# Hybrid decoder layer with a hierarchical MoE: the weight ring's last two places exchanged, the ninth chunk no longer held back, three gather buffers moved

## The chip, the cores and the metric

The kernel runs on one core of a Trainium2 chip. The time is the device time of one execution in microseconds. A core has five engines with instruction streams of their own: TensorE (PE), VectorE (DVE), ScalarE (ACT), GpSimd (POOL) and SyncE (SP). SyncE computes nothing here and issues DMAs. Sixteen DMA engines move data between HBM and the on-chip memory; SyncE's DMAs go through one queue (q1 in the profile) and GpSimd's through another (q0).

## What is computed

One layer for 512 prompt tokens and 8 sample tokens, all with 1024 features. A mixer with a recurrent and an attention branch gives `x1`; then comes a mixture of experts, with the top 1 of 4 groups and the top 2 of the 8 experts in it:

```
x1 = layer_norm(ALPHA * x + merged @ w_o, ln1_g, ln1_b)
g_logits = xf @ w_group + b_group                      # top 1 of 4
e_logits = (xf @ w_router + b_router)                  # 8 per group, top 2
...
def expert_block(args):
    xi, e = args
    h = jax.nn.silu(xi @ w_gate[e]) * (xi @ w_up[e])
    return h @ w_down[e]
...
y = layer_norm(ALPHA * x1 + ff, ln2_g, ln2_b)
```

All values are float32. Each of the 32 experts has three matrices of 2 MB (1024 x 512, 1024 x 512 and 512 x 1024), 201 MB together.

## The kernel before

The program is written out engine by engine, and all order between engines is made with semaphores. It has two stages around the change.

**The mixer** ends at about 504 us with the product `w_o`. Its result, before the norm, is `zT` (features on the partitions). TensorE transposes it into `zn`, which has the tokens on the partitions (semaphore `s_zt`), and multiplies it by the router's weights (`s_lg`, "logits"). ScalarE normalises the five token tiles in place (`s_x1` counts them), and GpSimd stores each to `x1_half` in HBM (`s_x1o` counts 16 for each store that has landed). Meanwhile VectorE works through the routing, a chain of small instructions that ends in tables: `s_oh10` counts slot one-hots, `s_tabc` the tables that are ready (the first is `tabG`, which tells which rows an expert gathers).

**The experts.** For expert e, GpSimd gathers the rows of its tokens from `x1_half` into one of four buffers `xg`, VectorE scales them by `g1` and `b1`, TensorE transposes them, VectorE copies the result to `xt`, and TensorE multiplies by gate and up (`gate_up`, in two halves), and by down (`down`) one expert later. The results are scattered to `ff_half`. Tables always cover 64 tokens per expert, as half rows.

**The weight ring.** The 96 weight chunks of 2 MB go through a ring of 11 places `slot[0]` to `slot[10]` of 16384 bytes per partition, at the bottom of on-chip memory. A chunk is half of gate and up together (two DMAs of 1 MB) or a whole down matrix. `load(n)` on SyncE issues chunk n; from n = 11 on it first waits until TensorE has read the chunk that lay there. So the first eleven loads depend on TensorE only through the mixer's buffers, which lie at the same addresses, and chunk 11 waits for the first half of expert 0's `gate_up`:

```
def load(n):
    if n >= RING:
        sp.wait_ge(*read_by(n - RING))
```

Of the places, `slot[8]` lies over `zT`, `slot[9]` and the lower part of `slot[10]` over the routing's temporaries (`rt(...)`, handed out from `oG` upwards), and the upper part of `slot[10]` over `zn`. The gather buffers `xg` lie above the ring, over the rows of `zn`, so they are cleared (`memset`) only after the stores of x1 have landed. SyncE issues its DMAs in program order, and a wait holds back all behind it.

Of the kernel before, what the change touches and what calls it, by code (L numbers as in the profile page):

```python
# [18 lines left out]
F32 = mybir.dt.float32  # L19
F32R = mybir.dt.float32r  # L20
BF16 = mybir.dt.bfloat16
U32 = mybir.dt.uint32
# [5 lines left out]
P = 128  # L28
# [6 lines left out]
TT = 5  # L35
# [4 lines left out]
NG, EPG = 4, 8  # L40
NE = NG * EPG
NL = NG + NE
# [3 lines left out]
CAP = 64  # L46
NOV = 16
NBLK = NE + NOV
# [4 lines left out]
NXG = 4  # L53
RING = 11
SLOT = 16384
# [88 lines left out]
def build(nc, A, O):  # L144
    ctx = ExitStack()
    with ctx:
        base = 16512

        def at(name, shape, dt, off):
            return nc.alloc_sbuf_tensor_at(name, shape, dt, offset=base + off)  # L150

        def sem(name):
            return ctx.enter_context(nc.semaphore(name))
# [5 lines left out]
        oE, oF, oG, oH, oI, oJ = 126720, 139840, 148224, 189184, 172800, 205568  # L159
# [80 lines left out]
        ro = [oG]  # L240

        def rt(name, shape, dt=F32):
            n = 1
            for s in shape[1:]:
                n *= s
            t = at(name, shape, dt, ro[0])
            ro[0] += (n * (2 if dt == BF16 else 4) + 31) // 32 * 32
            return t
        lg, lt = rt("lg", [P, TT, NL]), rt("lt", [P, TT, NL])
        lgG, lgE = lg[:, :, 0:NG], lg[:, :, NG:NL]  # L250
        io4 = rt("io4", [P, NG])
        io32 = rt("io32", [P, NE])
        ioM = rt("ioM", [P, TT, NE])
        io64 = rt("io64", [P, CAP])
        io48 = rt("io48", [P, NBLK])
        io16 = rt("io16", [P, NOV])
        tri = rt("tri", [P, P])
        triB = rt("triB", [P, P], BF16)
        oneB = rt("oneB", [P, P], BF16)
        tokv = rt("tokv", [P, 2, 2, TT])  # L260
        off = rt("off", [P, 1])
        w5 = [rt(f"w5{n}", [P, TT]) for n in range(5)]
        w10 = [rt(f"w10{n}", [P, 2, TT]) for n in range(6)]
        g20 = [rt(f"g20{n}", [P, TT, NG]) for n in range(2)]
        e320 = [rt(f"e320{n}", [P, 2 * TT, NE]) for n in range(2)]
        esel = rt("esel", [P, TT, NE])
        hot = rt("hot", [P, 2, TT, NE])
        hotB = rt("hotB", [P, TT, NE], BF16)
        cum = rt("cum", [P, 4, NE])
        ov16 = rt("ov16", [P, NOV, NE])  # L270
        bkE = rt("bkE", [P, 2 * TT, NBLK])
        tabG = at("tabG", [P, NBLK], U32, oK + 3040)
        tabD = at("tabD", [P, NBLK], U32, oK + 3232)
        tabW = at("tabW", [P, NBLK], F32, oK + 3424)
        ovT = at("ovT", [P, NOV + 1], I32, oK + 3616)
        ovf = at("ovf", [P, NOV + 1], F32, oK + 3712)
        rk = rt("rk", [P, 2 * TT, CAP])
        bk = rt("bk", [P, 2 * TT, 3, NBLK])
        assert ro[0] <= oI

        slot = [at(f"slot{n}", [P, 8, 512], F32, SLOT * n) for n in range(RING)]
        oX = RING * SLOT
        oX = RING * SLOT
        xt = [at(f"xt{n}", [P, 512], F32, oX + 2048 * n) for n in range(2)]
        gu = [at(f"gu{n}", [P, 512], F32, oX + 4096 + 2048 * n) for n in range(2)]
        xg = [at(f"xg{n}", [P, 512], F32, oX + 8320 + 2048 * n) for n in range(NXG)]
        g1, b1 = [at(n, [P, 512], F32, oX + 16512 + 2048 * k) for k, n in enumerate(("g1", "b1"))]
        sgm = [at(f"sgm{n}", [P, 4, CAP], F32, oX + 20608 + 1024 * n) for n in range(2)]
        hT = [at(f"hT{n}", [P, 4, CAP], F32, oX + 22656 + 1024 * n) for n in range(2)]
        idG = [at(f"idG{n}", [P, 1], U32, oX + 24704 + 32 * n) for n in range(NXG)]  # L290
        idD = [at(f"idD{n}", [P, 1], U32, oX + 24832 + 32 * n) for n in range(2)]

        f0 = [at(f"f0{n}", [P, D], F32, 4096 * n) for n in range(TT)]
        f1 = [at(f"f1{n}", [P, D], F32, 4096 * (TT + n)) for n in range(TT)]
# [59 lines left out]
        s_hot, s_pre, s_oh10, s_tab, s_tabc, s_tabo = sem("one_hots"), sem("ranks"), sem("slot_one_hots"), sem("tables"), sem("tables_kept"), sem("overflow_table")  # L354
# [69 lines left out]
        def read_by(n):  # L424

            e, c = CHUNKS[n]
            return (s_guh, s_gup, s_yp)[c], e + 1
# [7 lines left out]
        def _(sp):  # L435
# [59 lines left out]
# [4 lines that stand above are left out]
                chunk(CHUNKS[n][1], CHUNKS[n][0], slot[n % RING], s_wx[n % RING])  # L499

            def chunk(c, e, dst, signal):

                if c < 2:
                    for n, w in enumerate(("w_gate", "w_up")):
                        src = A[w][bass.ds(e, 1), c * (D // 2):(c + 1) * (D // 2), :].rearrange("e (p j) f -> p (e j f)", p=P)
                        sp.dma_start(dst[:, 4 * n:4 * n + 4, :].rearrange("p j f -> p (j f)"), src).then_inc(signal, 16)  # L506
                else:
                    src = A["w_down"][bass.ds(e, 1), :, :].rearrange("e (p j) d -> p (e j d)", p=P)
                    sp.dma_start(dst[:, :, :].rearrange("p a b -> p (a b)"), src).then_inc(signal, 16)  # L509
# [28 lines left out]
            load(7)  # L538
            sp.wait_ge(s_zt, 4)
            sp.wait_ge(s_lg, 1)  # L540
            sp.wait_ge(s_x1o, 16 * TT)
            load(8)
            sp.wait_ge(s_tabc, 4)
            for n, name in enumerate(("ln2_g", "ln2_b")):
                sp.dma_start(vec32[n * KT:(n + 1) * KT, :], A[name].rearrange("(k n) -> k n", n=P)).then_inc(s_l2, 16)
            load(9)
            load(10)

            for n in range(RING, 3 * NE - 1):
# [35 lines left out]
        def _(pool):  # L585
            gp = nc.gpsimd
            pc = [0]

            def link(ins):

                pc[0] += 1
                ins.then_inc(p_c, 1)
                pool.wait_ge(p_c, pc[0])
# [88 lines left out]
            pool.wait_ge(s_rcst, 10)  # L682
            gp.memset(off[CAP:P, :], float(FARAWAY + 1)).then_inc(s_rcst, 1)
            pool.wait_ge(s_rcst, 11)
            for m, n in enumerate(ORDER):
                pool.wait_ge(s_x1, m + 1)
                pool.dma_start(x1_rows[n * P:n * P + ROWS[n], :].rearrange("t (c n) -> t c n", c=4),
                               zn[m][P - ROWS[n]:P, :, :]).then_inc(s_x1o, 16)
            pool.wait_ge(s_x1o, 16 * TT)
            for j in range(NXG):  # L690
                link(gp.memset(xg[j][:, :], 0.0))
            pool.wait_ge(s_tabc, 1)

            def fetch(dst, index, signal):
# [1315 lines left out]
```

## Time and profile before

| | |
|---|---|
| median of 3 runs | 1030.9 us (1029.38 to 1034.28) |
| profiled execution, whole | 1030.14 us |
| its span (first to last instruction) | 1028.3 us |
| PE busy | 886.4 us, 86% of the span |
| DVE busy | 447.9 us, 44% |
| ACT busy | 280.7 us, 27% |
| POOL busy | 117.6 us, 11% |
| HBM read and written | 257.36 MB and 15.16 MB |

Times in the trace count from the start of the span. A row of a timeline has the start, the duration, the engine, the line of the kernel and the tiles that are written and read; in square brackets stand the engine's idle time before it and what ended it. "SPq" is SyncE's own sequence of DMA issues; such a row is the issue alone, not the transfer.

### The profile page before, as it was taken

The numbers are of one execution on the slowest core, as the hardware profiler recorded it, in microseconds if no ns is written. First come the engines' busy times: TensorE is split into PE (matmuls) and PEld (weight loads), VectorE is DVE, ScalarE is ACT, GpSimd is POOL, SyncE is SP. The second block draws the span as 40 slices with busy tenths as digits, with TensorE's granted clock in tenths as the row PEclk, the third lists the DMA queues.
The fourth block names the chain that finished last, engine by engine and source line by source line (L and its number), as shares of the span: only waits on it lengthen the run. The fifth ranks groups of instructions, "written<-read, shape, count | busy, mean of one in ns | idle before, by whom it ended". The sixth has DMA issues, their size and how long they took to land.

```text
span 1028.3 us, 14537 instructions
## 1 busy us (share of the span) xinstructions
PE 886.4 (86%) x5897; PEld 615.0 (60%) x5897; DVE 447.9 (44%) x922; ACT 280.7 (27%) x537; POOL 117.6 (11%) x202
## 2 busy tenths in 40 slices
PE   6899999899999999999749999997777877777870
PEld 6789999789899989998733333332332322322330
DVE  3865876774555645442462232332212212222207
ACT  3667544345344422211311111111010110110113
POOL 2000300000000010030130122211111111111110
PEclk9999999989999999999959999999999999999995
DMA  9324621212122232439389999999999999999946
GB/s 285 113 62 82 189 78 63 81 42 83 48 77 82 51 81 85 121 137 415 145 332 419 423 421 422 424 420 423 425 420 423 424 422 422 423 421 423 422 174 232
DMA packets 85957, 263.16 MB, mean 256 GB/s; under 512 B 28767, under 2 KB 59643, under 8 KB 65250
## 3 DMA queue, kind: packets, MB, share of 16 engines
q1 hardware_dynamic: 78850, 246.94, 61.9%
q0 software_dynamic: 7040, 15.28, 4.0%
q8 instruction: 47, 0.77, 0.3%
q14 instruction: 20, 0.16, 0.0%
HBM read 257.36 MB, written 15.16 MB: 265 GB/s over the span
## 4 chain that ended last, share of the span: by engine, by line
PE 43%; SPq 27%; DMA 13%; DVE 10%; ACT 3%; issue 3%; POOL 1%; POOLq 0%; DVEq 0%; ACTq 0%
PE ps L768 28%; SPq L506 22%; PE ps L1065 5%; SPq L509 4%; PE ps L1092 4%; DMA slot<-in_w_up 3%; DMA xg<-x_half,idG 3%; DMA ff_half<-xg,idD 2%; DMA raw<-in_w_o 2%; DMA raw<-in_w_in 1%; PE ps L894 1%; PE ps L884 1%; DVE rawL L1418 1%; PE ps L860 1%; DVE hL L1499 1%
## 5 line engine op out<-in xcount | busy, mean ns | idle before, releaser
L1065 PE MATMUL ps<-slot,xt 128*64 128x512 f32 x512 | 231.9, 600 | 47.6 <-DMA slot<-in_w_up 46.8
L1066 PE MATMUL ps<-slot,xt 128*64 128x512 f32 x512 | 232.4, 601 | 0.0
L1065 PEld LDWEIGHTS ps<-slot,xt 128*64 128x64 f32 x512 | 66.4, 137 | 184.4 <-issue 139.7
L768 PE MATMUL ps<-xTh,wh 128*128 128x260 f32 x704 | 147.0, 290 | 4.0 <-DVE rawL L1418 4.0
L768 PE MATMUL ps<-xTl,wh 128*128 128x260 f32 x704 | 143.1, 285 | 0.0
L768 PE MATMUL ps<-xTh,rawL 128*128 128x260 f32 x704 | 143.1, 285 | 0.0
L1092 PE MATMUL ps<-slot,hT 128*64 128x512 f32 x512 | 116.9, 597 | 19.1 <-issue 17.7
L1418 DVE TENSOR_TENSOR rawL<-raw,wh 128x1024 fp32r<-128x1024 f32 x68 | 84.1, 1240 | 81.7 <-ACT wh L1150 81.6
L768 PEld LDWEIGHTS ps<-xTh,wh 128*128 128x128 f32 x704 | 110.0, 192 | 9.9 <-issue 9.1
L768 PEld LDWEIGHTS ps<-xTl,wh 128*128 128x128 f32 x704 | 110.2, 191 | 0.0
L768 PEld LDWEIGHTS ps<-xTh,rawL 128*128 128x128 f32 x704 | 109.9, 191 | 0.0
L1341 ACT ACTIVATE gu<-ps 128x512 f32<-128x512 f32 x32 | 19.1, 597 | 284.7 <-PE ps L1066 284.7
L1150 ACT ACTIVATE wh<-raw 128x1024 fp32r<-128x1024 f32 x68 | 71.3, 1051 | 74.5 <-PE ps L768 47.9
L1899 DVE COPY xt<-ps 128x512 f32<-128x512 f32 x32 | 22.1, 691 | 148.9 <-PE ps L1049 148.9
L1092 PEld LDWEIGHTS ps<-slot,hT 128*64 128x64 f32 x512 | 38.0, 136 | 75.8 <-issue 72.9
L1906 DVE SCALAR_TENSOR_TENSOR xg<-ps,tabW,xg 128x512 f32<-128x512 f32 x32 | 24.0, 750 | 123.5 <-PE ps L1092 123.5
L1066 PEld LDWEIGHTS ps<-slot,xt 128*64 128x64 f32 x512 | 66.4, 137 | 0.0
L702 POOL DMA_INDIRECT ff_half<-xg,idD x32 | 32.8, 1025 | 171.4 <-DVE xg L1906 162.5
L1891 DVE TENSOR_TENSOR xg<-xg,g 128x512 f32<-128x512 f32 x32 | 22.1, 691 | 63.4 <-DMA xg<-x_half,idG 63.4
L1352 ACT ACTIVATE sgm<-ps 128x256 f32<-128x256 f32 x32 | 12.3, 383 | 136.4 <-PE ps L1077 136.4
L656 POOL TENSOR_TENSOR zT<-xTh,xTl 128x520 f32<-128x520 f32 x8 | 13.1, 1660 | 275.8 <-PE ps L894 206.9
L1235 ACT ACTIVATE sS<-sS,nm 128x256 f32<-128x256 f32 (+1 forms) x64 | 30.1, 471 | 46.1 <-DVE es L1538 46.1
(316 smaller groups left out, 1243.0 us busy)
## 6 DMA issues: line engine op xcount, KB each, us to landing
slot<-in_w_gate SPq DMA_DIRECT2D x64, 1024.0 KB, 30.5
slot<-in_w_up SPq DMA_DIRECT2D x64, 1024.0 KB, 31.5
slot<-in_w_down SPq DMA_DIRECT2D x31, 2048.0 KB, 33.0
raw<-in_w_in SPq DMA_DIRECT2D x18, 1024.0 KB, 5.2
raw<-in_w_in SPq DMA_DIRECT2D x16, 256.0 KB, 4.4
raw<-in_w_lru_out SPq DMA_DIRECT2D x4, 1024.0 KB, 4.8
raw<-in_w_attn_out SPq DMA_DIRECT2D x16, 256.0 KB, 4.5
raw<-in_w_o SPq DMA_DIRECT2D x4, 1024.0 KB, 5.2
```

The lines of the kernel that those rows point to most:

```text
L506: sp.dma_start(dst[:, 4 * n:4 * n + 4, :].rearrange("p j f -> p (j f)"), src).then_inc(signal, 16)
L509: sp.dma_start(dst[:, :, :].rearrange("p a b -> p (a b)"), src).then_inc(signal, 16)
L702: pool.indirect_dma_start(out=ff_half, out_offset=bass.IndirectOffsetOnAxis(ap=index[:, 0:1], axis=0), in_=src[:, :], in_offset=None, boun ...
L768: last = mm(out_of[:, a, 0:HT], w[:, k, :], x[:, k, a * HT:(a + 1) * HT], start=(k == 0 and n == 0), stop=(k == KT - 1 and n == 2))
L1065: mm(out[0:CAP, :], tokens, w[:, q, :], start=start, stop=stop)
L1066: last = mm(out[CAP:P, :], tokens, w[:, 4 + q, :], start=start, stop=stop)
L1092: last = mm(out[a * CAP:(a + 1) * CAP, :], h[:, q, :], w_down[:, 2 * q + a, :], start=(q == 0), stop=(q == 3))
L1150: sc.activation(whi(t), wcol(t, raw), ACT.Copy).then_inc(s_hi, 1)
L1235: sc.activation(sS[hh][:, j, lo:256], sS[hh][:, j, lo:256], ACT.Exp, bias=nm[:, hh, j:j + 1], accum_out=dn[:, hh, j:j + 1]).then_inc(s_ex, 1)
L1418: v.tensor_tensor(wcol(t, rawL), wcol(t, raw), whi(t).bitcast(F32), ALU.subtract).then_inc(s_lo, 1)
L1891: v.tensor_tensor(x, x, g1[:, :], ALU.mult).then_inc(s_xs, 1)
L1906: v.scalar_tensor_tensor(out=x, in0=bank[5 + e % 3], scalar=tabW[:, e:e + 1], in1=x, op0=ALU.mult, op1=ALU.add).then_inc(s_ye, 1)
```

## The change

Three things are edited.

1. The places of chunks 9 and 10 are exchanged in memory: `slot[9]` now lies at the tenth position from zero (over `zn` and some routing temporaries), `slot[10]` below it. The routing's temporaries are handed out in another order, so that those that die early lie under `slot[9]`.
2. On SyncE `load(8)` no longer waits for `s_x1o`. That wait, and one for the second slot one-hot, now stand ahead of `load(9)`, and `load(9)` stands ahead of the wait for the tables instead of behind it.
3. Three of the four `xg` buffers, `g1` and `b1` lie above the rows of `zn`. GpSimd clears those three ahead of the stores of x1, and the fourth after them.

```diff
+        cum = rt("cum", [P, 4, NE])
+        ...
+        io4 = rt("io4", [P, NG])
+        assert ro[0] <= 10 * SLOT
+        ro[0] = 10 * SLOT
+        lg, lt = rt("lg", [P, TT, NL]), rt("lt", [P, TT, NL])
...
-        slot = [at(f"slot{n}", [P, 8, 512], F32, SLOT * n) for n in range(RING)]
+        slot = [at(f"slot{n}", [P, 8, 512], F32, SLOT * (n if n < 9 else 19 - n)) for n in range(RING)]
...
-        xg = [at(f"xg{n}", [P, 512], F32, oX + 8320 + 2048 * n) for n in range(NXG)]
+        xg = [at(f"xg{n}", [P, 512], F32, oX + (15104 + 2048 * n if n < 3 else 12288)) for n in range(NXG)]
...
             sp.wait_ge(s_lg, 1)
+            load(8)
             sp.wait_ge(s_x1o, 16 * TT)
-            load(8)
+            sp.wait_ge(s_oh10, 2)
+            load(9)
             sp.wait_ge(s_tabc, 4)
             for n, name in enumerate(("ln2_g", "ln2_b")):
                 sp.dma_start(vec32[n * KT:(n + 1) * KT, :], A[name].rearrange("(k n) -> k n", n=P)).then_inc(s_l2, 16)
-            load(9)
             load(10)
...
             pool.wait_ge(s_rcst, 11)
+            for j in range(NXG - 1):
+                link(gp.memset(xg[j][:, :], 0.0))
             for m, n in enumerate(ORDER):
                 pool.wait_ge(s_x1, m + 1)
                 pool.dma_start(x1_rows[n * P:n * P + ROWS[n], :].rearrange("t (c n) -> t c n", c=4),
                                zn[m][P - ROWS[n]:P, :, :]).then_inc(s_x1o, 16)
             pool.wait_ge(s_x1o, 16 * TT)
-            for j in range(NXG):
-                link(gp.memset(xg[j][:, :], 0.0))
+            link(gp.memset(xg[NXG - 1][:, :], 0.0))
```

On SyncE's queue, from the chunk `slot7` on, before the change (the number behind a tile's name is that of its buffer, and in brackets stand the semaphores that the instruction waits for, by their long names: `x1_stored` is `s_x1o`, `tables_kept` is `s_tabc`):

```order
L509 DMA slot7_185<-in_w_down 128x4096
L506 DMA slot8_186<-in_w_gate 128x2048 [waits x1_stored,logits,z_T]
L506 DMA slot8_186<-in_w_up 128x2048
L545 DMA vec32_131<-in_ln2_g 8x128 [waits tables_kept]
L545 DMA vec32_131<-in_ln2_b 8x128
L506 DMA slot9_187<-in_w_gate 128x2048
L506 DMA slot9_187<-in_w_up 128x2048
L509 DMA slot10_188<-in_w_down 128x4096
L506 DMA slot0_178<-in_w_gate 128x2048 [waits gate_up_half]
```

The same place of SyncE's queue with the change (`slot_one_hots` is `s_oh10`):

```order
L511 DMA slot7_185<-in_w_down 128x4096
L508 DMA slot8_186<-in_w_gate 128x2048 [waits logits,z_T]
L508 DMA slot8_186<-in_w_up 128x2048
L508 DMA slot9_187<-in_w_gate 128x2048 [waits slot_one_hots,x1_stored]
L508 DMA slot9_187<-in_w_up 128x2048
L549 DMA vec32_131<-in_ln2_g 8x128 [waits tables_kept]
L549 DMA vec32_131<-in_ln2_b 8x128
L511 DMA slot10_188<-in_w_down 128x4096
L508 DMA slot0_178<-in_w_gate 128x2048 [waits gate_up_half]
```

The wait for x1 has moved from chunk 8 to chunk 9, and chunk 9 has passed the two small loads and their wait for the tables. Chunk 10 stays where it was.

On GpSimd, from its last constant to the first gather, before the change:

```order
L683 MEMSET off_149 64x1 [waits router_constants]
L687 DMA x1_half<-znp_124 32x1x256 [waits x1_ready,router_constants]
L687 DMA x1_half<-znp_124 512x1x256 [waits x1_ready] x4
L691 MEMSET xg0_193 128x512 [waits x1_stored]
L691 MEMSET xg1_194 128x512 [waits pool_order]
L691 MEMSET xg2_195 128x512 [waits pool_order]
L691 MEMSET xg3_196 128x512 [waits pool_order]
L710 COPY idG0_203<-tabG_171 128x1 [waits tables_kept,pool_order]
L696 DMA xg0_193<-x1_half,idG0_203 128x512 [waits gather_index]
```

The same place on GpSimd with the change:

```order
L686 MEMSET off_141 64x1 [waits router_constants]
L689 MEMSET xg0_203 128x512 [waits router_constants]
L689 MEMSET xg1_204 128x512 [waits pool_order]
L689 MEMSET xg2_205 128x512 [waits pool_order]
L692 DMA x1_half<-znp_124 32x1x256 [waits x1_ready,pool_order]
L692 DMA x1_half<-znp_124 512x1x256 [waits x1_ready] x4
L695 MEMSET xg3_206 128x512 [waits x1_stored]
L714 COPY idG0_197<-tabG_173 128x1 [waits tables_kept,pool_order]
L700 DMA xg0_203<-x1_half,idG0_197 128x512 [waits gather_index]
```

Three memsets have moved ahead of the five stores; one is left between the stores' landing and the first gather.

## Rows read from the trace of the kernel before

**Rows 1.** The page: DMA busy in tenths, in 40 slices of the span

```profile
DMA  9324621212122232439389999999999999999946
```

**Rows 2.** Windows: stretch, its length, busy us by engine, PEclk, DMA share, GB/s

```profile
523.00:524.00 1.00, 0.01 (x2) 0.01 (x2) 0.93 (x4) 0.00 (x0) 0.00 (x0) 0.50 0.33 127
524.00:525.00 1.00, 1.00 (x20) 1.00 (x20) 0.92 (x4) 0.00 (x0) 0.00 (x0) 0.50 0.03 12
526.00:527.00 1.00, 0.37 (x8) 0.21 (x4) 0.51 (x3) 0.00 (x0) 0.88 (x3) 0.50 0.95 147
528.00:529.00 1.00, 1.00 (x18) 1.00 (x16) 0.97 (x3) 0.00 (x0) 0.27 (x1) 0.50 0.97 410
532.00:533.00 1.00, 0.00 (x0) 0.00 (x0) 0.21 (x1) 0.00 (x0) 0.20 (x2) 0.50 0.38 82
539.00:540.00 1.00, 1.00 (x5) 0.24 (x4) 0.00 (x0) 0.00 (x0) 0.00 (x0) 0.60 1.18 492
544.00:545.00 1.00, 1.00 (x7) 0.17 (x3) 0.00 (x0) 0.00 (x0) 0.00 (x0) 1.00 0.66 262
560.00:975.00 415.00, 351.79 (x1616) 132.30 (x1613) 104.47 (x172) 45.69 (x86) 69.71 (x114) 1.00 1.01 422
```

**Rows 3.** The chain that ended last: start, us, what

```profile
950.67 30.25 DMA slot<-in_w_up
```

**Rows 4.** Timeline of SyncE's DMA issues

```profile
507.79 0.59 SPq L509 DMA_DIRECT2D slot<-in_w_down  x1
525.15 0.33 SPq L506 DMA_DIRECT2D slot<-in_w_gate  x1
532.29 0.35 SPq L506 DMA_DIRECT2D slot<-in_w_gate  x1
541.65 0.33 SPq L506 DMA_DIRECT2D slot<-in_w_gate  x1
```

**Rows 5.** Timeline of TensorE: the last matmuls of the logits

```profile
506.33 1.20 PE L955 MATMUL ps<-wrG,zT 128*128 128x36 f32 x10
```

**Rows 6.** The stores of x1: ns min/median/max, first and last start, forms

```profile
L687 POOL DMA_DIRECT2D x_half<-znp x5: 625/711/767, 512.2 to 516.4; - x5
```

**Rows 7.** Timeline of GpSimd, from the first store to gather 2

```profile
512.21 1.52 POOL L687 DMA_DIRECT2D x_half<-znp  x2 [4.96 <-ACT znp L1331]
525.11 2.28 POOL L691 MEMSET xg<- 128x512 f32 x4 [8.05 <-DMA x_half<-znp]
527.45 0.30 POOL L710 COPY idG<-tabG 128x1 uint32<-128x1 uint32 x1
528.73 1.14 POOL L696 DMA_INDIRECT xg<-x_half,idG  x1 [0.98 <-POOL idG L710]
...
533.06 1.33 POOL L696 DMA_INDIRECT xg<-x_half,idG  x1 [0.85 <-POOL idG L710]
```

**Rows 8.** DMA queues, 598 to 599 us: packets, MB, share of 16 engines

```profile
q1 hardware_dynamic: 43, 0.30, 72.3%
q0 software_dynamic: 41, 0.13, 32.6%
```

**Rows 9.** Timelines of VectorE and TensorE: table, first gathered tile, first weights

```profile
526.49 0.27 DVE L1866 TENSOR_SCALAR tabG<-ps,off 128x48 uint32<-128x48 f32 x1 [1.08 <-PE ps L1027]
532.79 0.69 DVE L1891 TENSOR_TENSOR xg<-xg,g 128x512 f32<-128x512 f32 x1 [1.20 <-DMA xg<-x_half,idG]
536.17 1.12 PE L1065 MATMUL ps<-slot,xt 128*64 128x512 f32 x1 [0.78 <-DVE xt L1899]
```

**Rows 10.** DMA issues (last figure: us to landing): gathers 0, 2 and 3

```profile
xg<-x_half,idG POOLq DMA_INDIRECT x1, 4.0
xg<-x_half,idG POOLq DMA_INDIRECT x1, 7.7
xg<-x_half,idG POOLq DMA_INDIRECT x1, 8.3
```

**Rows 11.** The page's groups: busy us, mean ns of one | idle before, releaser

```profile
L1065 PE MATMUL ps<-slot,xt 128*64 128x512 f32 x512 | 231.9, 600 | 47.6 <-DMA slot<-in_w_up 46.8
```

More of the change, by code:

```diff
@@ L248, in rt @@
             return t
[L249 to L253, printed above, removed]
         io64 = rt("io64", [P, CAP])
@@ L256, in build @@
         io16 = rt("io16", [P, NOV])
-        tri = rt("tri", [P, P])
-        triB = rt("triB", [P, P], BF16)
-        oneB = rt("oneB", [P, P], BF16)
         tokv = rt("tokv", [P, 2, 2, TT])
@@ L264, in build @@
         g20 = [rt(f"g20{n}", [P, TT, NG]) for n in range(2)]
+        cum = rt("cum", [P, 4, NE])
+        ov16 = rt("ov16", [P, NOV, NE])
+        bkE = rt("bkE", [P, 2 * TT, NBLK])
+        rk = rt("rk", [P, 2 * TT, CAP])
+        bk = rt("bk", [P, 2 * TT, 3, NBLK])
+        io32 = rt("io32", [P, NE])
+        io4 = rt("io4", [P, NG])
+        assert ro[0] <= 10 * SLOT
+        ro[0] = 10 * SLOT
+        lg, lt = rt("lg", [P, TT, NL]), rt("lt", [P, TT, NL])
+        lgG, lgE = lg[:, :, 0:NG], lg[:, :, NG:NL]
+        ioM = rt("ioM", [P, TT, NE])
+        tri = rt("tri", [P, P])
+        triB = rt("triB", [P, P], BF16)
+        oneB = rt("oneB", [P, P], BF16)
         e320 = [rt(f"e320{n}", [P, 2 * TT, NE]) for n in range(2)]
@@ L268, in build @@
         hotB = rt("hotB", [P, TT, NE], BF16)
-        cum = rt("cum", [P, 4, NE])
-        ov16 = rt("ov16", [P, NOV, NE])
-        bkE = rt("bkE", [P, 2 * TT, NBLK])
+        assert ro[0] <= oI
         tabG = at("tabG", [P, NBLK], U32, oK + 3040)
@@ L276, in build @@
         ovf = at("ovf", [P, NOV + 1], F32, oK + 3712)
-        rk = rt("rk", [P, 2 * TT, CAP])
-        bk = rt("bk", [P, 2 * TT, 3, NBLK])
-        assert ro[0] <= oI
-        slot = [at(f"slot{n}", [P, 8, 512], F32, SLOT * n) for n in range(RING)]
+        slot = [at(f"slot{n}", [P, 8, 512], F32, SLOT * (n if n < 9 else 19 - n)) for n in range(RING)]
         oX = RING * SLOT
@@ L285, in build @@
         gu = [at(f"gu{n}", [P, 512], F32, oX + 4096 + 2048 * n) for n in range(2)]
-        xg = [at(f"xg{n}", [P, 512], F32, oX + 8320 + 2048 * n) for n in range(NXG)]
[L287 to L291, printed above, removed]
+        sgm = [at(f"sgm{n}", [P, 4, CAP], F32, oX + 8192 + 1024 * n) for n in range(2)]
+        hT = [at(f"hT{n}", [P, 4, CAP], F32, oX + 10240 + 1024 * n) for n in range(2)]
+        idG = [at(f"idG{n}", [P, 1], U32, oX + 14336 + 32 * n) for n in range(NXG)]
+        idD = [at(f"idD{n}", [P, 1], U32, oX + 14464 + 32 * n) for n in range(2)]
+        xg = [at(f"xg{n}", [P, 512], F32, oX + (15104 + 2048 * n if n < 3 else 12288)) for n in range(NXG)]
+        g1, b1 = [at(n, [P, 512], F32, oX + 21248 + 2048 * k) for k, n in enumerate(("g1", "b1"))]
         f0 = [at(f"f0{n}", [P, D], F32, 4096 * n) for n in range(TT)]
```

## The prediction

> **What bounds the kernel now.** I read the page first. Its DMA line stays at 9 from slice 20 to slice 38 [rows 1]: from about 545 us to the landing of the last expert weights the DMA engines never rest. The windows give the rate, 422 GB/s over 560 to 975 us at a DMA share of 1.01 [rows 2]. The chain that ended last closes with SyncE issuing weights, then 30.25 us in which one `w_up` chunk lands [rows 3]; the matmuls that wanted it start as it lands. TensorE has idle time in this stage; a faster engine there buys nothing. So the end of the kernel is the end of the weight stream, and the stream ends later by each microsecond in which, since the experts' first chunks were issued, the DMA engines had nothing to move.
>
> Next I looked for those microseconds, between 504 and 546 us, in windows of 1 us [rows 2]. The engines are full to 523, nearly empty in 524 to 526 (12 GB/s at 524), full again from about 526.5, low at 532 (82 GB/s), and full up to one dip at 544 (share 0.66). That is some 4 us of rest in these windows. SyncE's rows say why [rows 4]: the ninth chunk, `load(8)`, is issued at 525.15, after the stored rows of x1, and the tenth at 532.29, after the tables.
>
> The dip at 544 is the row that matters most. There chunk 10, the eleventh and last that the empty ring takes, runs out, and chunk 11 takes over. Chunk 11 needs slot 0 free. TensorE freed it at 541.65 [rows 4], and an issue into an idle queue moves its first bytes about 1.5 us later (issue at 525.15, 147 GB/s in 526 to 527, so a start near 526.6) [rows 2, 4]. Chunk 11 could thus have started at 543.1, and it started at about 544.6, behind its predecessor. So before the change the ring and TensorE are within 1.5 us of each other. From here on the stream starts at the later of two times: when the first eleven chunks are in, and 1.5 us after slot 0 is free.
>
> **Part by part.** *`load(8)` without the x1 wait.* Its last wait is then the logits, whose matmuls end at 506.33 + 1.20 = 507.53 [rows 5]; SyncE is at this place after `load(7)`, issued at 507.79 for 0.59 us [rows 4]. So it issues near 508.4, 16.7 us earlier. It moves 2 x 1024 KB, 2.10 MB, which at the 410 GB/s of a full row [rows 2] is 5.1 us of all engines. By itself this fills the rest at 524 to 526 and part of that at 532. But the first eleven chunks then end some 5 us earlier, near 539.5, and the stream can use only 1.5 us of it unless slot 0 comes free earlier.
>
> *What load(8) meets.* The x1 rows are issued by GpSimd from 512.2 to 516.4 [rows 6] on the other queue, and land by 525.1, when the first memset behind them starts [rows 7]. Now 2.10 MB of `slot8` stand in SyncE's queue in the same stretch. How two full queues share the engines is seen at 598 to 599 us: 41 packets of GpSimd's queue and 43 of SyncE's in the same microsecond, 32.6% and 72.3% of the time [rows 8]. They alternate, about packet for packet. The x1 rows are 2.13 MB (520 rows of 4 KB), in smaller packets than the weights'; alternating, the weights finish first and the rows of x1 end last, when all of both is moved. The engines were busy until 523.4 without `slot8` (the 0.33 share of 523 to 524), so they end 5.1 us later less the small gaps filled, 4.9 us: `s_x1o` at 530.0. Bounds: 0 if x1's queue went first, 5.3 if nothing is filled.
>
> *The memsets.* Four took from 525.11 to 527.39 after the stores (2.28 us). Three go ahead of the stores, where GpSimd had idled 4.96 us [rows 7], so there they cost nothing; if that cover were gone, 1.7 us. One is left, a quarter of that, 0.57 us. The gather's indices need `tabG`, ready at 526.49 + 0.27 = 526.76 [rows 9], before either. Before, gather 0 was issued at 528.73, 3.62 us after the memsets began. Now it is x1's landing + 0.57 + 1.34 (copy and its wait, from the memsets' end at 527.39 to 528.73) [rows 7], so 530.0 + 1.9 = 531.9: 3.2 us later. Moving the memsets gives back 1.7, the late x1 rows take 4.9.
>
> *Gather 0 and the queue beside it.* It landed in 4.0 us; gathers 2 and 3, issued from 533.06 on beside `load(9)` and `load(10)`, in 7.7 and 8.3 [rows 7, 10]. Now `load(9)` is issued at `s_x1o`, 530.0 (its other wait, the second one-hot, is long over), and keeps the engines full for 5.1 us from about 531.5; `load(10)` follows after the tables at about 532.4 as before. Gather 0 at 531.9 stands between two full chunks. I take 8.0, the mean of the two gathers in that place, so 4.0 us more; the bounds are 4.0 and 8.3. Together gather 0 lands 3.2 + 4.0 = 7.2 us later.
>
> *From there to the stream.* Scaling, transpose and `xt` copy follow as before: xg at 532.79, first weight matmul at 536.17, slot 0 free at 541.65 [rows 4, 9]. The first half of the expert ran partly at the lower clock (granted 0.50, 1.2 GHz, until 539, 0.60 in that microsecond, 1.00 after) [rows 2], with matmuls of 1.12 us at 536.17 against a mean of 0.60 over all of them [rows 9, 11]. I keep that share. Slot 0 comes free at 548.8, the stream starts at 550.3 instead of 544.6: 5.7 us later. The eleven chunks are in by about 544 (from 531.5, 10.2 us for two chunks and up to 2.5 for four gathers of at most 262 KB), so they don't set it. The exchange of places 9 and 10 adds no instruction; the other edits move addresses, and the tables' chain on VectorE is the same instruction for instruction. On SyncE the two small ln2 loads now stand behind `load(9)`; nobody waits for them before the end.
>
> **Sum.** -16.7 us on an issue that is not the limit; +4.9 on x1; -1.7 for memsets; +4.0 for the gather; less the 1.5 us by which slot 0 was early. 5.7 us on the profiled 1030.14 us is 1035.8; that execution lies 0.8 below the median of 1030.9, so 1036.6, rounded to 1036.5.
>
> The Trainium skill ("DMA: Bandwidth & Descriptors", Anatomy of one DMA) has a GpSimd DMA at about 2.0 us plus its bytes over 436 GB/s. For a gather of at most 128 half rows (262 KB) that is an estimate of 2.6 us beside any traffic. The rows disagree by 1.4 us at the quiet gather and 5 us at the loaded ones. By the Trainium skill's figure the sum would be 3.2 - 1.4 - 1.5 = +0.3 us, 1031.2.
>
> **Rivals.**
> *A gather that stays quick.* x1 is late, but gather 0 still lands in 4.0 us, since `load(10)` isn't yet queued when it is issued. For it: gather 0 before was issued while `load(8)` was under way too. Against: there the chunk was nearly through. Slot 0 at 544.9, stream at 546.4: +1.8, 1032.7. The Trainium skill's fixed price, above, is this rival in its extreme.
> *Not slower: the rows of x1 go ahead.* If the engines serve GpSimd's queue first, x1 still lands at 525.1. Then gather 0 waits for `tabG` alone and is issued at 528.1, 0.65 earlier; slot 0 at 541.0, stream at 542.5, -2.1 us: 1028.8. Against it speaks the even split at 598. This decides from one point: as long as gather 0 lands less than 1.5 us later than before, the change loses nothing.
> *TensorE stays longer at the lower clock.* It starts after a longer pause. Of the first half of expert 0, the part from about 539.6 to 541.65 ran at the upper clock; at the lower one its 2.05 us take 1.12/0.60 as long, 1.8 us more: +7.5, 1038.4, and 1038.7 with the slower gather.
> *A real gain* needs expert 0 to begin earlier than the tables allow; I see no row for it beyond the 2.1 us.
>
> **Numbers.** Forecast 0.60, quick gather 0.15, x1 ahead 0.15, clock 0.05, unforeseen gain 0.05. The forecast's own range is +3.9 to +6.7 by its bounds (x1 at 530.0 +- 0.3, gather 6.5 to 8.3 us), 1034.8 to 1037.6. For 8 in 10 the range goes from 1029.0 (nearly the x1-ahead case) to 1038.8. A measurement here tells about 0.5%, 5.2 us, from no change. Of the forecast's 0.60, nearly 0.4 lies over 1036.1, and the clock case too: slower 0.46. Faster by 0.5% (below 1025.7): 0.07. Within: 0.47.
>
> **What would show it.** `slot8`'s issue near 508.4 right behind `slot7`; the memset after the stores at about 530 instead of 525.1 (x1 term); gather 0 issued near 531.9 and landing in about 8 us; the first expert matmul near 543 and slot 0 free near 549; a rest of some 6 us in the DMA windows just ahead of chunk 11, and none at 524; then 422 GB/s to the end. It is wrong if the memset starts before 527, or if gather 0 lands before 535.

## The result

Five runs of the changed kernel have a median of 1038.89 us (1038.41 to 1041.41), five of the kernel before 1030.91 us (1029.38 to 1036.95). The ratio is 1.0069, with a 95% interval of 1.0043 to 1.0095: slower by 0.7%. (A ratio here is worked out from all runs and need not be the quotient of the medians, which lie 8.0 us apart.) The forecast was slower, by 5.6 us. The median lies 1.3 us over the forecast's own range (1034.8 to 1037.6) and 0.1 us over the wide one (1029.0 to 1038.8).

In the profiled execution the span is 1036.7 us. The page of the changed kernel has this DMA line, to set against [rows 1]:

```profile
DMA  9324622212212324349486999999999999999946
```

Counted from 0, the slices from 22 on are as before, and slice 21 (544 to 570 us) has gone from 9 to 6; slice 19 is 4 instead of 3. The slices before those belong to the mixer; some differ by a tenth or two. Windows of 1 us and more in this stretch (the columns of [rows 2]) show where:

```profile
530.00:531.00 1.00, 1.00 (x18) 1.00 (x16) 0.76 (x4) 0.00 (x0) 0.00 (x0) 0.50 0.04 16
531.00:532.00 1.00, 0.82 (x12) 0.53 (x8) 0.13 (x1) 0.00 (x0) 0.67 (x2) 0.50 0.00 0
545.00:551.00 6.00, 5.58 (x16) 1.71 (x18) 1.66 (x3) 0.00 (x0) 0.00 (x0) 0.60 0.00 0
551.00:552.00 1.00, 1.00 (x8) 0.34 (x6) 0.00 (x0) 0.00 (x0) 0.00 (x0) 1.00 0.00 0
560.00:975.00 415.00, 353.23 (x1624) 132.48 (x1620) 106.10 (x174) 46.13 (x87) 70.15 (x114) 1.00 1.01 421
```

The rest that stood at 524 to 526 has not gone. It is at 530 to 532 now, behind the stores as before, because chunk 9 still waits for them. And a new one stands from 545 to 552, 7 us without a byte, where the kernel before had a dip of a third of a microsecond at 544. From 560 on the rate is nearly the same, 421 against 422 GB/s.

SyncE's issues of the changed kernel name the cause, set against [rows 4]:

```profile
505.27 0.33 SPq L508 DMA_DIRECT2D slot<-in_w_gate  x1
...
509.34 0.37 SPq L508 DMA_DIRECT2D slot<-in_w_gate  x1
...
531.24 0.33 SPq L508 DMA_DIRECT2D slot<-in_w_gate  x1
...
533.30 0.35 SPq L511 DMA_DIRECT2D slot<-in_w_down  x1
551.29 0.35 SPq L508 DMA_DIRECT2D slot<-in_w_gate  x1
```

Chunk 8 is issued at 509.34 instead of 525.15, 16 us earlier. Chunk 9 is issued at 531.24, behind the stores. Chunk 11, the first that needs TensorE to free a place, goes out at 551.29 instead of 541.65. GpSimd's and VectorE's rows, set against [rows 7, 9], lie between:

```profile
508.22 1.70 POOL L689 MEMSET xg<- 128x512 f32 x3
...
531.27 0.52 POOL L695 MEMSET xg<- 128x512 f32 x1 [13.30 <-DMA x_half<-znp]
533.02 1.15 POOL L700 DMA_INDIRECT xg<-x_half,idG  x1 [0.98 <-POOL idG L714]
```

```profile
527.40 0.27 DVE L1870 TENSOR_SCALAR tabG<-ps,off 128x48 uint32<-128x48 f32 x1 [1.08 <-PE ps L1031]
542.03 0.69 DVE L1895 TENSOR_TENSOR xg<-xg,g 128x512 f32<-128x512 f32 x1 [9.54 <-DMA xg<-x_half,idG]
```

GpSimd's wait for the rows of x1 has grown from 8.05 to 13.30 us, and VectorE's wait for the first gather from 1.20 to 9.54 us. The table `tabG` stands ready at 527.7 and is not what gather 0 waits for.

The mixer ahead of this stage does not end at the same time in every execution. In the profiled one before, SyncE issued `slot6`, the first thing that it does when the mixer's last product is done, at 504.36:

```profile
504.36 0.33 SPq L506 DMA_DIRECT2D slot<-in_w_gate  x1
```

Over all the traces of this study it lies between there and 510.89. So from here on times "after slot6" count from that row in each trace. The table has them for all kernels, with one trace for each. "Memset" is the start of the one behind the stores, which shows when x1 had landed; "took" is from gather 0's issue to VectorE's first use of it; "slot 0 free" is chunk 11's issue; "last" is the landing of the last `w_up`, the end of a row like this one of the changed kernel (to set against [rows 3]):

```profile
960.13 30.31 DMA slot<-in_w_up
```

The kernel before was timed again beside each group of kernels. Its medians were 1031.56 us beside a1 to a4, 1031.34 beside b1 to b3 and 1030.95 beside c1 and c2, and each ratio is to the runs of its own group.

| kernel | memset | gather 0 issued | took | slot 0 free | last | median us | ratio to before |
|---|---|---|---|---|---|---|---|
| before | 20.75 | 24.37 | 4.06 | 37.29 | 476.56 | 1030.91 | 1 |
| changed | 26.00 | 27.75 | 9.01 | 46.02 | 485.17 | 1038.89 | 1.0069 (1.0043 to 1.0095) |
| a1 load(8) alone freed | 25.92 | 29.42 | 6.69 | 45.59 | 483.54 | 1038.59 | 1.0081 (1.0064 to 1.0099) |
| a2 load(8) held | 20.73 | 23.75 | 7.43 | 40.04 | 479.23 | 1034.0 | 1.0023 (1.0013 to 1.0034) |
| a3 load(9) behind gather 0 | 25.92 | 27.67 | 2.96 | 39.89 | 481.01 | 1036.25 | 1.0046 (1.0033 to 1.0059) |
| a4 memsets and layout alone | 20.89 | 23.75 | 4.95 | 38.64 | 477.73 | 1031.55 | 1.0006 (0.9991 to 1.0022) |
| b1 stores in SyncE's queue | 20.98 | 23.75 | 7.17 | 40.22 | 479.44 | 1034.52 | 1.0026 (1.0012 to 1.0040) |
| b2 the same, load(9) later | 21.07 | 23.74 | 3.41 | 36.34 | 475.84 | 1030.64 | 0.9999 (0.9983 to 1.0015) |
| b3 half of chunk 8 early | 23.30 | 25.29 | 7.33 | 42.54 | 481.89 | 1036.18 | 1.0052 (1.0031 to 1.0072) |
| c1 chunk 10 in rows of 8 KB | 25.77 | 27.52 | 7.47 | 43.76 | 483.05 | 1038.92 | 1.0078 (1.0061 to 1.0095) |
| c2 load(10) behind gather 0 | 25.93 | 27.67 | 6.18 | 43.27 | 482.15 | 1036.28 | 1.0058 (1.0041 to 1.0074) |

### The profile page after: what moved, and what is told of

It is laid out like the page before. It is cut to its first block, busy times and chain, and to the rows that moved or that the text cites. A ratio compares the mean times of both kernels' runs of the same rounds, so it can differ in the third digit from the quotient of the medians.

```text
span 1036.7 us, 14538 instructions
## 1 busy us (share of the span) xinstructions
PE 891.0 (86%) x5897; PEld 619.2 (60%) x5897; DVE 447.7 (43%) x922; ACT 280.9 (27%) x537; POOL 117.1 (11%) x202
## 4 chain that ended last, share of the span: by engine, by line
PE 40%; SPq 27%; DMA 14%; DVE 11%; issue 4%; ACT 4%; POOL 1%; POOLq 0%; DVEq 0%; ACTq 0%
PE ps L772 27%; SPq L508 22%; SPq L511 4%; DMA xg<-x_half,idG 4%; PE ps L1069 3%; PE ps L1096 3%; DMA ff_half<-xg,idD 3%; DMA slot<-in_w_up 3%; DMA raw<-in_w_o 2%; DMA raw<-in_w_in 1%; PE ps L898 1%; DVE rawL L1422 1%; PE ps L864 1%; PE ps L888 1%; DVE hL L1503 1%
```

## The experiments

The theory under test is the prediction's: chunk 8, issued early, shares the engines with the rows of x1 and makes them late, and the first gather, now late, stands beside full chunks and takes twice its time.

**a1: load(8) alone.** The kernel before, with one line moved.

```diff
+            load(8)
             sp.wait_ge(s_x1o, 16 * TT)
-            load(8)
```

> The kernel before, with load(8) alone freed from the wait for the stored rows of x1; memsets, layout and load(9) as before. My theory (the early chunk 8 makes the rows of x1 land late, and gather 0, now later, stands beside two full chunks): chunk 8 issued near 508.5, first memset behind the stores near 530.4 instead of 525.1, gather 0 issued near 534.0 and landing in 8 to 9 us, slot 0 free near 551 to 552, 8 to 10 us slower than before (1039 to 1041). Rival (freeing load(8) is harmless, the loss comes from load(9) ahead of the tables and the gather): x1 lands at 525 to 526, within 1 us of before.

The memset starts 25.92 us after slot6, as forecast, and the kernel is as slow as the changed one, as far as the intervals of the two ratios tell. So this one line is enough for the loss. Its parts are others: with four memsets behind the stores the gather is issued 1.7 us later than in the changed kernel, and it took 2.3 us less. At 6.69 us it missed the 8 to 9 that I gave. Slot 0 was free at 550.57 instead of 551 to 552, and the median of 1038.59 us lies just under the 1039 to 1041 that I gave. GpSimd's timeline:

```profile
530.90 2.28 POOL L691 MEMSET xg<- 128x512 f32 x4 [13.21 <-DMA x_half<-znp]
534.40 1.14 POOL L696 DMA_INDIRECT xg<-x_half,idG  x1 [0.98 <-POOL idG L710]
```

**a2: load(8) held, all else as changed.**

```diff
-            load(8)
             sp.wait_ge(s_x1o, 16 * TT)
+            load(8)
             sp.wait_ge(s_oh10, 2)
             load(9)
```

> The changed kernel, with load(8) back behind the stored rows of x1; load(9) still right behind it, ahead of the tables, and the three memsets ahead of the stores. My theory: x1 lands at 525.1 again, gather 0 is issued near 528.1, bound by tabG, but lands in 7.7 to 9 us because chunks 8 and 9 are both queued: at 536 to 537 instead of 532.8, slot 0 free at 545 to 546, 2 to 3 us slower than before (1033 to 1034), 5 us faster than the changed kernel. Rival (x1's lateness costs nothing, all the loss is the gather beside full chunks): as slow as the changed kernel, 1039. Rival (only the late x1 costs): as fast as before or 1 us faster.

GpSimd's timeline of this kernel:

```profile
526.15 0.52 POOL L695 MEMSET xg<- 128x512 f32 x1 [8.02 <-DMA x_half<-znp]
527.99 0.20 POOL L714 COPY idG<-tabG 128x1 uint32<-128x1 uint32 x1 [1.31 <-DVE tabG L1870]
529.17 1.55 POOL L700 DMA_INDIRECT xg<-x_half,idG  x1 [0.98 <-POOL idG L714]
```

x1 lands on time, the gather's copy now waits for `tabG` (the bracket names it), and the gather took 7.43 us with chunks 8 and 9 queued. The time is 4.9 us below the changed kernel's and 0.23% over before. Both single-cause rivals fall: early chunk 8 costs about 5 us, and a gather that is on time but stands beside two chunks about 2.5. The 5 us are not the late rows alone: next to the changed kernel the gather is issued 4.0 us earlier and took 1.6 us less.

**a3: load(9) behind gather 0.**

```diff
             sp.wait_ge(s_oh10, 2)
+            sp.wait_ge(s_g[0], 16)
             load(9)
```

> The changed kernel, with load(9) (and so the ln2 loads and load(10)) waiting until gather 0 has landed; load(8) early. My theory: x1 lands late as in the changed kernel (near 530.4), gather 0 is issued near 532.1 and now lands in 2.8 to 4.0 us at 535 to 536, slot 0 free near 544.5; but chunks 9 and 10 start only near 537 and end near 548.5, so the stream is then held by the ring: 3.5 to 5 us slower than before (1034.5 to 1036), 3 to 4.5 us faster than the changed kernel. Rival (the gather's long landing has another cause than the weights beside it, such as its own late start): gather 0 still takes 8 to 9 us and the kernel is slower than the changed one.

The gather, issued as late as in the changed kernel but with an empty queue beside it, took 2.96 us. Its rows in the timelines of GpSimd and VectorE:

```profile
533.50 1.15 POOL L701 DMA_INDIRECT xg<-x_half,idG  x1 [0.98 <-POOL idG L715]
```

```profile
536.46 0.69 DVE L1896 TENSOR_TENSOR xg<-xg,g 128x512 f32<-128x512 f32 x1 [3.38 <-DMA xg<-x_half,idG]
```

So the 9 us of the changed kernel come from the weights beside it and not from its lateness. Slot 0 was free 39.89 us after slot6, only 2.6 us later than before, but chunks 9 and 10 started late: the ring became the limit, as expected, and the kernel is 0.46% slower than before.

**a4: memsets and layout alone.** SyncE's order is that of the kernel before.

```diff
-            load(8)
             sp.wait_ge(s_x1o, 16 * TT)
-            sp.wait_ge(s_oh10, 2)
-            load(9)
+            load(8)
             sp.wait_ge(s_tabc, 4)
...
+            load(9)
             load(10)
```

> The changed kernel's layout and memsets, with SyncE's order of before: load(8) behind the stored rows of x1, load(9) behind the tables. My theory: gather 0 issued 0.65 us earlier than before (bound by tabG), landing in about 4 us, slot 0 free 0.65 us earlier; the ring's last chunk ends when it did, so the time is that of before within 1 us (1030 to 1031). Rival (the new layout or the early memsets cost something of their own): over 2 us slower than before.

The gather is issued 0.62 us earlier, but took 0.9 us longer, perhaps because more of chunk 8 was still to come, and the first half expert took 6.55 us against 5.48. So slot 0 was free 1.35 us later and not 0.65 earlier, within the 1.5 us that the ring leaves. The time is not to be told from that of before (0.9991 to 1.0022). That speaks against the rival's 2 us and more. A smaller cost is not excluded: in the trace the last `w_up` landed 1.2 us later than before, and the section on the prediction comes back to that.

**b1: the stores in SyncE's queue.** The changed kernel, with the five stores taken from GpSimd's program.

```diff
+            for m, n in enumerate(ORDER):
+                sp.wait_ge(s_x1, m + 1)
+                sp.dma_start(x1_rows[n * P:n * P + ROWS[n], :].rearrange("t (c n) -> t c n", c=4),
+                             zn[m][P - ROWS[n]:P, :, :]).then_inc(s_x1o, 16)
             load(8)
             sp.wait_ge(s_x1o, 16 * TT)
```

> The changed kernel, with the five stores of x1 issued by SyncE, in its own queue ahead of load(8), instead of by GpSimd; load(8) follows them without a wait, load(9) as in the changed kernel. My theory (the x1 rows were late because two queues share the engines packet by packet): in one queue the rows go first, the memset behind them starts 20 to 21 us after slot6's issue as before (26.0 in the changed kernel), although chunk 8 is queued at once. Gather 0 is then issued at 23.7 us after slot6's issue (bound by tabG) and lands in 7 to 9 us beside chunks 8 and 9: slot 0 free near 40, 2 to 3 us slower than before, 5 us faster than the changed kernel. Rival (chunk 8's bytes delay the rows wherever they stand): memset at 25 to 26, as slow as the changed kernel.

Chunk 8 stands right behind the stores, issued 7.6 us before they have landed, and the memset starts 20.98 us after slot6, as before. So the same bytes queued behind the rows, in their own queue, do not delay them. The edit moves the issue of chunk 8 too, from 4.07 us after slot6 to 13.40, and no run separates the two. In the changed kernel the 70 packets of SyncE's queue in 519 to 521 us have 0.53 MB, so mostly 8 KB each, where the 46 in 517 to 519, with 0.75 MB, are chunk 7's of 16 KB. Its chunk 8 thus began to move near 519, 13.7 us after slot6, and the earlier issue gave it little lead. The gather took 7.17 us and the time is that of a2, as the theory has it. The timelines of SyncE and of GpSimd:

```profile
518.16 6.09 SPq L545 DMA_DIRECT2D x_half<-znp  x5
524.29 2.26 SPq L508 DMA_DIRECT2D slot<-in_w_gate  x1
```

```profile
531.87 0.52 POOL L695 MEMSET xg<- 128x512 f32 x1 [16.34 <-DMA x_half<-znp]
```

(Slot6 was issued at 510.89 in this execution.)

**b2: the same, load(9) a little later.** The version to which the experiments point: early chunk 8 behind the rows, and the gather ahead of chunk 9. The new wait (`s_ig` counts the copied gather indices) is over when GpSimd has issued gather 0.

```diff
             sp.wait_ge(s_oh10, 2)
+            sp.wait_ge(s_ig, 2)
             load(9)
```

> As the kernel with the stores on SyncE, and load(9) waits besides until gather 0 has been issued (gather 1's index is copied). My theory: chunk 8 has nearly landed when gather 0's packets come, so it lands in 4 to 5 us; slot 0 is free 36.9 to 38 us after slot6's issue (37.3 before), chunks 9 and 10 are in by about 39.5 (40.2 before): 0 to 1.5 us faster than before, 1029.5 to 1031.5. Rival (the gather is slowed by any chunk behind it, also one issued a microsecond later): it lands in 7 to 9 us and the kernel is 2 to 3 us slower than before.

Its timelines of GpSimd and of VectorE:

```profile
528.68 1.54 POOL L701 DMA_INDIRECT xg<-x_half,idG  x1 [0.98 <-POOL idG L715]
```

```profile
531.97 0.21 DVE L1889 TENSOR_SCALAR tabF<-ps 128x48 f32<-128x48 f32 x1
532.09 0.68 DVE L1896 TENSOR_TENSOR xg<-xg,g 128x512 f32<-128x512 f32 x1
```

The gather took 3.41 us, and VectorE's row has no wait in brackets any more: it comes straight from the last table, `tabF`, so a still quicker gather 0 would bring nothing here. Slot 0 was free 36.34 us after slot6, 1 us earlier than before. The last weights landed 0.7 us earlier. The ratio is 0.9999 (0.9983 to 1.0015): that is not to be told from the kernel before. The median is 0.8% under the changed kernel's.

**b3: half of chunk 8 early.** Its gate half is issued where `load(8)` stood, the up half behind `s_x1o`. (`part8` issues one of the two DMAs of `load(8)`.)

```diff
-            load(8)
+            part8(0, "w_gate")
             sp.wait_ge(s_x1o, 16 * TT)
+            part8(1, "w_up")
```

> The changed kernel, with only the gate half of chunk 8 (1 MB) issued early and its up half behind the stored rows of x1. My theory (the lateness of the x1 rows is the time of the bytes that share the engines with them): half the bytes, half the lateness, so the memset behind the stores starts 23.3 us after slot6's issue (20.8 before, 26.0 in the changed kernel); gather 0 is issued at 25.2 to 25.4, lands in 7.5 to 9 us, slot 0 free near 42 to 43.5: 4.5 to 6 us slower than before, 2 to 3 us faster than the changed kernel. Rival (a fixed price for any weights beside the stores): memset at 26, as slow as the changed kernel.

GpSimd's timeline:

```profile
529.15 0.52 POOL L700 MEMSET xg<- 128x512 f32 x1 [10.60 <-DMA x_half<-znp]
```

The memset starts at 23.30: 2.55 us late for 1 MB, against 5.25 for 2 MB. The lateness is the time of the bytes beside the stores. The gather took 7.33 us, a little under the 7.5 to 9 that I gave; slot 0 and the time are as expected.

**c1: chunk 10 in rows of 8 KB.** Two DMAs of 1 MB each instead of one of 2 MB.

```diff
-            load(10)
+            w10 = A["w_down"][CHUNKS[10][0], :, :].rearrange("(p j) d -> p (j d)", p=P)
+            for h in range(2):
+                sp.dma_start(slot[10][:, 4 * h:4 * h + 4, :].rearrange("p a b -> p (a b)"),
+                             w10[:, 2048 * h:2048 * (h + 1)]).then_inc(s_wx[10], 16)
```

> The changed kernel, with chunk 10 (a down matrix) loaded by two DMAs of 1 MB whose rows are 8 KB long instead of one of 2 MB with rows of 16 KB; the same bytes at the same place. My theory (the gather's packets take turns with the weights' packets, so their length sets its price: it took 9.0 us in the changed kernel, where the first gather's packets met chunk 10, and 6.7 to 7.4 where they met rows of 8 KB): gather 0 lands in 7.0 to 7.7 us, slot 0 free near 44 to 45 us after slot6's issue (46.0 in the changed kernel), 1 to 2 us faster than the changed kernel. Rival (only that chunks are queued counts, not their rows): 8.7 to 9.3 us, the time of the changed kernel.

GpSimd's and VectorE's rows in their timelines:

```profile
537.89 1.15 POOL L703 DMA_INDIRECT xg<-x_half,idG  x1 [0.98 <-POOL idG L717]
```

```profile
545.36 0.69 DVE L1898 TENSOR_TENSOR xg<-xg,g 128x512 f32<-128x512 f32 x1 [7.76 <-DMA xg<-x_half,idG]
```

The gather took 7.47 us instead of 9.01, as the theory gave, and in the trace slot 0 is free 2.3 us earlier and the last `w_up` lands 2.1 us earlier after slot6. The median of its four runs does not show it: 1038.92 us, ratio 1.0078 (1.0061 to 1.0095), where 1 to 2 us less than the changed kernel were expected. That part missed: the trace shows the gather's price up to the end of the weight stream, the times do not.

**c2: load(10) behind gather 0.**

```diff
+            sp.wait_ge(s_g[0], 16)
             load(10)
```

> The changed kernel, with load(10) waiting until gather 0 has landed; load(9) still ahead of the gather. My theory (gather 0 takes turns with what is queued when its packets come; chunk 9 ends some 3.5 us after the gather's issue): it lands in 5 to 6.5 us instead of 9.0, slot 0 free near 42 to 44 us after slot6's issue, 2 to 4 us faster than the changed kernel, still 4 to 6 us slower than before. Rival (chunk 9 alone, issued ahead of the gather, makes the whole price): 8 to 9 us and no gain on the changed kernel.

The gather took 6.18 us with chunk 9 alone beside it, and the median is 2.6 us under the changed kernel's, the ratio 1.0058 against 1.0069 with intervals that overlap. The gather's time and slot 0 are within the expectation. The gain in time is not clear of noise; the rival falls by the gather's own time.

## Why the prediction came out as it did

**The bound** was right: the weight stream ends the kernel, and its start is slot 0 or the ring. a3 shows the one limit (slot 0 free only 2.6 us later than before, last landing late by 4.5 us), the changed kernel the other. The page's nines run from slice 21 to slice 37, counted from 0, and not from 20 to 38; nothing hangs on it.

**The issue, -16.7 us**: measured 16.7 (4.07 us after slot6 instead of 20.79). As forecast, it is not the limit.

**x1 late by 4.9 us**: measured 5.25 (20.75 to 26.00). The alternation read at 598 us [rows 8] holds in the stretch itself. The changed kernel's queues from 519 to 527 us, packets, MB and share:

```profile
q1 hardware_dynamic: 293, 2.23, 66.6%
q0 software_dynamic: 290, 1.06, 32.9%
```

293 packets of weights and 290 of the other queue. b3 confirms it by half the bytes, and b1 agrees.

**Memsets, -1.7 us**: from the memset's start to gather 0 it is 1.75 us instead of 3.62, so -1.9. They cost nothing where they went (1.70 us in a pause of GpSimd).

**Gather, +4.0 us**: measured +4.95. This is the term of the sum that was mis-sized. Gathers 2 and 3 of the kernel before were no measure for gather 0 here. The length of the rows beside it counts: 7.47 us when chunk 10's rows are 8 KB and 9.01 when they are 16 KB (c1), 6.18 with chunk 9 alone (c2), 2.96 with nothing (a3).

The price has two parts. From 533 to 537 us, the first 4 us after its issue, the changed kernel moved packets of SyncE's queue alone:

```profile
q1 hardware_dynamic: 220, 1.67, 99.4%
```

The first packet of GpSimd's queue started 4.4 us after the gather's issue in the changed kernel, in c1 too, 4.5 us after it in c2 and 1.7 us in a3. Why it waits so long no run shows. What is left is 4.6, 3.1, 1.7 and 1.2 us. In that part the queues take turns; the changed kernel's, from 540 to 543 us:

```profile
q1 hardware_dynamic: 75, 1.23, 96.4%
q0 software_dynamic: 73, 0.13, 11.4%
```

Gather 0 of a3 moved 80 packets in all (533.5 to 536.4 us), 5 for each engine if they are spread evenly. A packet of 16 KB holds an engine for 0.62 us (96.4% of 48 us over 75), one of 8 KB for about 0.29 us (99.4% of 64 us over 220). Five turns behind the longer ones cost 1.6 us more by this estimate, and c1 against the changed kernel shows 1.54.

The flat price that I quoted from the Trainium skill ("DMA: Bandwidth & Descriptors", Anatomy of one DMA), 2.6 us by estimate, fits the quiet gather of a3 within 0.4 us, and none of the loaded ones. Its formula has no term for what else is queued, and "beside any traffic" was my reading of it.

**From the gather to slot 0, no change**: 0.4 us more. Of the first weights to chunk 11's issue it is 5.87 us (545.42 to 551.29) against 5.48. The granted clock was 0.50 up to 549 and 0.58 in the microsecond from there, by the changed kernel's window:

```profile
549.00:550.00 1.00, 1.00 (x6) 0.31 (x4) 0.00 (x0) 0.00 (x0) 0.00 (x0) 0.58 0.00 0
```

The low level (1.2 GHz) held for a little more of this half expert, some 4.4 us against 3.6 (0.60 at 539, [rows 2]). Over the traces this piece took between 5.4 and 6.6 us; the clock rival of 1.8 us did not come.

**Less 1.5 us of slack**: right within 0.1 us. The stream began about 7.3 us later (1.5 us after 551.29, by 505.27, against 544.6 by 504.36), where slot 0 was free 8.7 later.

**Put at nothing**: the last `w_up` landed 8.6 us later after slot6, so the stream itself took 1.3 us longer, at 421 instead of 422 GB/s. The prediction had the rate unchanged and the new addresses free, and this is the largest single piece of what it lacks. By the traces it goes with the new layout and not with the execution. a4, whose stream starts as before, has 1.2 us of it. Where slot 0 sets the start, the time from slot 0 to the last `w_up` is "last" less "slot 0 free" in the table. It is 437.95 us in a1, which has the old layout, and 438.88 to 439.35 us in the six with the new one (changed, a2, b1, b3, c1, c2). That is one trace for each kernel, the ratio of a4 does not tell it from nothing, and why addresses should count stays open.

So of the 2.9 us that the sum lacks against 8.6, the stream makes 1.3, the gather 0.95, its way to slot 0 0.4 and x1 0.35, less 0.2 for the memsets, to rounding. No term changed its sign, and but for those 0.2 us no errors cancelled. The mixer ended 0.9 us later and the tail was 1.1 us shorter. 0.9 + 8.6 - 1.1 = 8.4, the difference of the spans. The upper end of the forecast's own range does not come out of its bounds either: 5.7 + 0.3 + 0.3 is 6.3 and not 6.7.

Of the rivals, a gather that stays quick fell (9.01 us), and that the rows of x1 go ahead fell too: they take turns. Its break-even, 1.5 us of lateness of gather 0, agrees with b1 and a2, where VectorE begins on it 2.5 and 2.8 us late (0.26 and 0.23% slower), and with a4, 0.3 us late and the same.

## What to carry to other kernels

A rest of the DMA engines is worth filling only if what ends next is the transfer; here it was already within 1.5 us of TensorE's first release, and the first release hung on two small transfers, the stored rows and the gather. Before a bulk load is moved earlier, list the small transfers on other queues that it will run beside and what waits for them: the stored rows paid by the bytes beside them (2.55 us for 1 MB, 5.25 for 2 MB), the gather by a wait before its first packet and by the length of the packets that it takes turns with. Where a bulk load should follow a small transfer, putting both in one queue kept the rows ahead without a wait in b1. That is a matter of time alone: no run shows that data which depend on each other would be safe without one.

## What the runs showed of the hardware

- Two DMA queues with work share the engines packet for packet (293 against 290 in 8 us), so that the queue with the longer packets gets the larger share of the time: 66.6% against 32.9%.
- A gather of the same rows took 2.96 us beside an empty queue, 6.2 beside one chunk, 6.7 to 7.5 where it met mostly rows of 8 KB, and 9.0 with rows of 16 KB. Its first packet started 4.3 to 4.7 us after its issue in the changed kernel, a1, a2, b1, b3, c1 and c2, and 1.7 us beside the empty queue of a3.
- The same stores, issued by SyncE, cost 6.09 us of its issue time for five and landed at the same time after slot6 (20.98 against 20.75) as from GpSimd. They moved in smaller packets: 771 with 0.77 MB in 525 to 527 us of b1, against 231 with 0.82 MB in 519 to 521 us of the kernel before.
